# Parameter and constant tables allocated ahead of the weight rings, x and h: every one of those tiles moves by 32 bytes modulo 128

## The chip, the cores and the metric

The kernel runs on one core of one Trainium2 chip. The metric is the device time of one execution in microseconds; each number for a kernel is a median over runs on the chip, and the profile is one profiled execution of the same program.

## What is computed

The reference is two transformer-like blocks over 256 positions and 2048 channels, all in float32. The first has three mixers side by side (pooling, a long convolution done as a Fourier transform, chunked spatial gating) and a feed-forward part; the second has banded attention, an RWKV-7 delta rule and attention to a memory, merged by gates. Cut to the products that take nearly all of the time:

```python
p = rmsnorm(x, norm_mix) @ w_in
x = x + concat([y_a, y_b, y_c]) @ w_out
up = dwconv3(rmsnorm(x, norm_ffn) @ ffn_w_up)
x = x + (silu(gate) * val) @ ffn_w_down
x = rmsnorm(x, norm_final)
proj = rms_norm(x, norm_g) @ w_in_2            # heads, queries, gates
mk, mv = split(rms_norm(mem, mem_norm_g) @ w_mem_kv)
merged = sum(sigmoid(g_m) * (y_m @ w_up_m) for m in (a, b, c))
out = x + merged @ w_o
```

## The kernel before

Activations lie transposed in SBUF, channels over the 128 partitions, 256 positions along each partition. Weights come from HBM as 736 "units" of 512 KB (128 partitions x 1024 floats), each good for 8 tiles of 128x128. SyncE loads unit after unit into a ring of four buffers `raw`. For each unit ScalarE writes the high half `w_hi` (`split`, line 909: a copy rounded to fp32r), VectorE writes `w_lo = raw - w_hi` (line 1316), and TensorE multiplies: for each weight tile three matmuls of 128x128 weights with 256 moving columns, high by high, high by low and low by high, so 24 matmuls a unit. All matmuls are recorded at line 417. Each matmul has its own weight load, which TensorE runs beside the matmul before it (PEld in the profile). The ring's order is fixed in the code: ScalarE waits until TensorE has used the unit four back, VectorE for ScalarE, TensorE for VectorE, SyncE for VectorE.

What multiplies the weights (the moving operand) lies in one of two places:

- **`h_hi`, `h_lo`**, the normed input in two halves: tiles of their own. Used for w_in, ffn_w_up, w_in_2 with its heads, queries and gates: 3 x 4016 matmuls.
- **the shared area** (called the arena from here on), one stretch of SBUF from `arena_at` on in which `place` puts tiles that take turns: `y_hi/y_lo` (for w_out, 3 x 256 matmuls), `m_hi/m_lo` (ffn_w_down, 3 x 704), `mh_hi/mh_lo` (w_mem_kv, 3 x 256), `ya_hi/ya_lo` (the three up-projections, 3 x 384), `mg_hi/mg_lo` (w_o, 3 x 256). The float32 tiles of the delta rule (`m_a`, `m_Q`, `s_...`) are there too.

The tiles are allocated one behind the other along a partition, each from the next multiple of 32 bytes. `par` has 637 floats (2548 bytes) and `con` 1092 (4368 bytes). The byte addresses that follow (start of the tile within a partition, and that modulo 128) are:

| tiles | before | mod 128 | after | mod 128 |
|---|---|---|---|---|
| `raw0` (first of the rings) | 16512 | 0 | 23456 | 32 |
| `w_hi0` | 32896 | 0 | 39840 | 32 |
| `w_lo0` | 49280 | 0 | 56224 | 32 |
| `x` | 65664 | 0 | 72608 | 32 |
| `h_hi`, `h_lo` | 82048, 98432 | 0 | 88992, 105376 | 32 |
| `par`, `con` | 114816, 117376 | 0 | 16512, 19072 | 0 |
| arena | 121760 | 32 | 121760 | 32 |

All moving tiles in the arena start at a multiple of 1024 bytes from its start, and a unit's or tile's parts are 512 or 1024 bytes apart, so each of these matmuls has the offset modulo 128 of its row in the table.

Of the kernel before, what the change touches and what calls it, by code (L numbers as in the profile page):

```python
# [26 lines left out]
P = 128  # L27
# [44 lines left out]
NPAR = _at  # L72
# [11 lines left out]
NCONST = _at  # L84
# [82 lines left out]
def build(nc, a):  # L167
    out_ap = a["out"]
    with ExitStack() as ctx:
        def sb(name, shape, dt=F32):  # L170
            return ctx.enter_context(nc.sbuf_tensor(name, shape, dt))
# [4 lines left out]
        banks = [ctx.enter_context(nc.psum_tensor(f"bank{i}", [P, 512], F32)) for i in range(8)]  # L176


        raw = [sb(f"raw{i}", [P, UK, UN]) for i in range(RING)]
        w_hi = [sb(f"w_hi{i}", [P, UK, UN], F32R) for i in range(RING)]  # L180
        w_lo = [sb(f"w_lo{i}", [P, UK, UN], F32R) for i in range(RING)]
        x = sb("x", [P, KT, T])
        h_hi = sb("h_hi", [P, KT, T], F32R)
        h_lo = sb("h_lo", [P, KT, T], F32R)
        par = sb("par", [P, NPAR])
        con = sb("con", [P, NCONST])
        arena_at = nc.sbuf_base
        arena_at = (arena_at + 31) // 32 * 32
        usable = nc.sbuf_usable_end - arena_at
# [1949 lines left out]
```

How the kernel before makes its waits and increments, by code:

```python
        @block.gpsimd  # L387
        def _(pool):
            for dst, src in ((feat[:, :], "feat"), (fw1[:, :], "fw1"), (fw2[:, :], "fw2")):
                pool.dma_start(dst, a[src]).then_inc(filt_in, 16)
            pool.wait_ge(landed[1], 16)
            for dst, src in ((fw3[:, :], "fw3"), (decay[:, :, :], "decay"), (dft[:, :, :, :], "dft")):
                pool.dma_start(dst, a[src]).then_inc(tables_in, 16)
            pool.wait_ge(free_early, 1)
            for dst, src in ((ws[:, :, :], "ws"), (pw[:, :, :], "pw"), (bs[:, :], "bs")):
                pool.dma_start(dst, a[src]).then_inc(mixer_in, 16)
            pool.wait_ge(free_inv, 1)
            pool.dma_start(inv[:, :, :], a["inv"]).then_inc(inv_in, 16)
            pool.wait_ge(free_lora, 1)
            pool.dma_start(lora[:, :], a["lora"]).then_inc(lora_in, 16)
            with pool.Fori(0, HEADS_A) as g:
                pool.wait_ge(bias_used, g + 1)
                pool.dma_start(bias_t[:, :], a["bias"][g]).then_inc(bias_in, 16)
            pool.wait_ge(free_mem, 1)
            for c in range(4):
                cs = slice(4 * c, 4 * c + 4)
                pool.dma_start(memx[:, cs, :], a["memT"][:, cs, :]).then_inc(mem_in[c], 16)
# [10 lines left out]
            def unit(bank, k0, hi, lo, first, last, tiles=2, fresh=True):  # L419
                slot = next(slots) % RING
                pe.wait_ge(split_done, n.next("split"))
                o = p2(bank)
                for kk in range(UK):
                    for t in range(tiles):
```

## Time and profile before

| | |
|---|---|
| median of 3 runs | 2538.08 us (2537.49 to 2540.97) |
| profiled execution, first to last instruction | 2537.8 us (the page gives no other time of its own) |
| TensorE busy | 2455.0 us, 97% |
| VectorE, ScalarE busy | 1534.1 us, 60%; 1185.9 us, 47% |
| DMA | 400.39 MB, mean 158 GB/s |

Busy time of an engine counts stretches in which at least one of its instructions ran. TensorE's matmuls overlap in the profile (one lasts 0.28 us and the next begins 0.12 us after it), so the length of one is not its cost; the distance between two starts is.

### The profile page before, as it was taken

The page shows a single profiled execution, that of the slowest core. Times are in us where ns is not written, and L with a number is a line of the kernel's source. Part 1 is how long each engine was busy: PE and PEld are TensorE (multiplying, and loading weights), DVE is VectorE, ACT ScalarE, POOL GpSimd, SP SyncE. Part 2 cuts the span into 40 slices and gives each one's busy share as a digit, 9 for nine tenths or more (in the row PEclk, how much of TensorE's full clock was granted, in tenths as well). Part 3 has the DMA queues.
Part 4 walks back from the last instruction along what each step waited for, and adds up shares of the span by engine and source line. Part 5 has one row for each costly group of instructions (what it writes and reads, how often), then busy time and mean ns, then how long its engine had stood idle before and what let it go on. Part 6 is the DMA issues. An engine that isn't in the chain of part 4 may idle for free.

```text
span 2537.8 us, 51128 instructions
## 1 busy us (share of the span) xinstructions
PE 2455.0 (97%) x19960; PEld 2413.6 (95%) x19960; DVE 1534.1 (60%) x2050; ACT 1185.9 (47%) x1502; POOL 12.8 (1%) x27
## 2 busy tenths in 40 slices
PE   6999998999999999997899999999999999999999
PEld 6898997999999999996899999999999999999999
DVE  6456566666555666566866666766576454544454
ACT  5343335665434666434444445444465443434433
POOL 0000000000000000000000000000000000000000
PEclk9999898999999999998999999999999999999999
DMA  6353354555554555554333333333355355555554
GB/s 233 130 180 116 129 187 132 188 170 194 183 186 167 183 181 189 179 185 147 117 119 112 109 120 111 119 123 104 118 175 173 125 184 179 185 176 175 184 187 160
DMA packets 110145, 400.39 MB, mean 158 GB/s; under 512 B 12394, under 2 KB 12421, under 8 KB 109904
## 3 DMA queue, kind: packets, MB, share of 16 engines
q1 hardware_dynamic: 108000, 391.00, 46.4%
q0 software_dynamic: 2032, 7.67, 0.9%
q8 instruction: 97, 1.59, 0.3%
q14 instruction: 16, 0.13, 0.0%
HBM read 396.52 MB, written 2.10 MB: 157 GB/s over the span
## 4 chain that ended last, share of the span: by engine, by line
PE 92%; DVE 5%; issue 1%; ACT 1%; DMA 0%; DVEq 0%; SPq 0%; ACTq 0%
PE bank L417 91%; DVE w_lo L1316 1%; ACT w_hi L909 1%; DVE scratch L1365 1%; PE bank L611 0%; DVE s_k L1365 0%; DVE h_lo L1362 0%; DMA x<-in_xT 0%; DVE cum L1362 0%; DVE root L1404 0%; DVE ping L1362 0%; DVE s_t L1362 0%; DVE qr L1807 0%; DVE acc L1362 0%; DVE s_t L1369 0%
## 5 line engine op out<-in xcount | busy, mean ns | idle before, releaser
L1316 DVE TENSOR_TENSOR w_lo<-raw,w_hi 128x1024 fp32r<-128x1024 f32 x736 | 892.0, 1224 | 803.8 <-ACT w_hi L909 797.5
L909 ACT ACTIVATE w_hi<-raw 128x1024 fp32r<-128x1024 f32 x736 | 770.7, 1057 | 1018.7 <-PE bank L417 999.5
L417 PE MATMUL bank<-h_hi,w_hi 128*128 128x256 f32 x4016 | 1163.3, 290 | 36.6 <-DVE h_lo L1362 15.0
L417 PE MATMUL bank<-h_lo,w_hi 128*128 128x256 f32 x4016 | 1141.0, 284 | 0.0
L417 PE MATMUL bank<-h_hi,w_lo 128*128 128x256 f32 x4016 | 1140.8, 284 | 0.0
L417 PEld LDWEIGHTS bank<-h_hi,w_hi 128*128 128x128 f32 x4016 | 775.6, 193 | 47.0 <-issue 24.4
L417 PEld LDWEIGHTS bank<-h_lo,w_hi 128*128 128x128 f32 x4016 | 775.9, 193 | 3.3 <-issue 2.2
L417 PEld LDWEIGHTS bank<-h_hi,w_lo 128*128 128x128 f32 x4016 | 775.0, 193 | 0.0
L417 PE MATMUL bank<-m_hi,w_lo 128*128 128x256 f32 x704 | 197.8, 281 | 0.0
L417 PE MATMUL bank<-m_hi,w_hi 128*128 128x256 f32 x704 | 197.1, 280 | 0.0
L417 PE MATMUL bank<-m_lo,w_hi 128*128 128x256 f32 x704 | 195.7, 278 | 0.0
L417 PEld LDWEIGHTS bank<-m_hi,w_hi 128*128 128x128 f32 x704 | 132.4, 188 | 0.0
L417 PEld LDWEIGHTS bank<-m_lo,w_hi 128*128 128x128 f32 x704 | 132.4, 188 | 0.0
L417 PEld LDWEIGHTS bank<-m_hi,w_lo 128*128 128x128 f32 x704 | 132.2, 188 | 0.0
L417 PE MATMUL bank<-ya_hi,w_lo 128*128 128x256 f32 x384 | 107.9, 281 | 0.0
L417 PE MATMUL bank<-ya_hi,w_hi 128*128 128x256 f32 x384 | 107.6, 280 | 0.0
L417 PE MATMUL bank<-ya_lo,w_hi 128*128 128x256 f32 x384 | 106.8, 278 | 0.0
L1365 DVE SCALAR_TENSOR_TENSOR conv_o<-bank,par,conv_o 128x255 f32<-128x255 f32 x176 | 76.7, 478 | 6.5 <-DVE conv_o L1365 3.3
L417 PE MATMUL bank<-mh_hi,w_hi 128*128 128x256 f32 x256 | 74.5, 291 | 5.1 <-DVE mh_lo L1362 3.4
L417 PEld LDWEIGHTS bank<-ya_hi,w_hi 128*128 128x128 f32 x384 | 72.3, 188 | 0.0
L417 PEld LDWEIGHTS bank<-ya_lo,w_hi 128*128 128x128 f32 x384 | 72.3, 188 | 0.0
L417 PE MATMUL bank<-mh_hi,w_lo 128*128 128x256 f32 x256 | 72.2, 282 | 0.0
(414 smaller groups left out, 2820.2 us busy)
## 6 DMA issues: line engine op xcount, KB each, us to landing
raw<-in_units SPq DMA_DIRECT2D x736, 512.0 KB, 3.4
x<-in_xT SPq DMA_DIRECT2D x4, 512.0 KB, 5.8
memx<-in_memT POOLq DMA_DIRECT2D x4, 512.0 KB, 7.2
out_y<-obuf SPq DMA_DIRECT2D x8, 256.0 KB, 4.3
bias_t<-in_bias POOLq DMA_DIRECT2D x8, 192.0 KB, 2.9
dft<-in_dft POOLq DMA_DIRECT2D x1, 1024.0 KB, 7.6
decay<-in_decay POOLq DMA_DIRECT2D x1, 768.0 KB, 5.6
con<-in_con SPq DMA_DIRECT2D x1, 546.0 KB, 7.8
```

What stands on the lines that cost most here:

```text
L417: return pe.matmul(out, lhsT, rhs, start=start, stop=stop, skip_group_check=True)
L909: return act.activation(out, in_, ACT.Copy, scale=scale)
L1316: dve.tensor_tensor(w_lo[slot][:, :, :], raw[slot][:, :, :], w_hi[slot][:, :, :].bitcast(F32), ALU.subtract).then_inc(split_done, 1)
L1365: return dve.scalar_tensor_tensor(out, x_, s, y_, op0, op1)
```

## The change

Two lines move to the head of the allocation. No instruction, wait or transfer is added, removed or moved: on each of the five engines the order of instructions is the same in both kernels. What differs is the address of the rings, of `x`, `h_hi`, `h_lo`, and of the two tables. The total size of what stands ahead of the arena is the same, so the arena starts where it did.

```diff
@@ build @@
+        par = sb("par", [P, NPAR])
+        con = sb("con", [P, NCONST])
         raw = [sb(f"raw{i}", [P, UK, UN]) for i in range(RING)]
         w_hi = [sb(f"w_hi{i}", [P, UK, UN], F32R) for i in range(RING)]
         w_lo = [sb(f"w_lo{i}", [P, UK, UN], F32R) for i in range(RING)]
         x = sb("x", [P, KT, T])
         h_hi = sb("h_hi", [P, KT, T], F32R)
         h_lo = sb("h_lo", [P, KT, T], F32R)
-        par = sb("par", [P, NPAR])
-        con = sb("con", [P, NCONST])
         arena_at = nc.sbuf_base
         arena_at = (arena_at + 31) // 32 * 32
```

## Rows read from the trace of the kernel before

**Rows 1.** The page: span, busy time, clock by slices, chain that ended last.

```profile
span 2537.8 us, 51128 instructions
PE 2455.0 (97%) x19960; PEld 2413.6 (95%) x19960; DVE 1534.1 (60%) x2050; ACT 1185.9 (47%) x1502; POOL 12.8 (1%) x27
...
PEclk9999898999999999998999999999999999999999
...
PE 92%; DVE 5%; issue 1%; ACT 1%; DMA 0%; DVEq 0%; SPq 0%; ACTq 0%
```

**Rows 2.** Waits of PE, ACT and SP's queue: total us, times, longest.

```profile
PE bank L417 <- DVE h_lo L1362: 15.0, 2, 8.0
PE bank L417 <- DVE w_lo L1316: 7.2, 5, 2.5
...
ACT w_hi L909 <- PE bank L417: 999.5, 567, 13.3
...
SPq L891 <- DVE w_lo L1316: 2055.1, 732, 26.6
```

**Rows 3.** Groups of matmuls by form: busy us, mean ns of one.

```profile
L417 PE MATMUL bank<-h_lo,w_hi 128*128 128x256 f32 x4016 | 1141.0, 284 | 0.0
...
L417 PE MATMUL bank<-m_lo,w_hi 128*128 128x256 f32 x704 | 195.7, 278 | 0.0
...
L417 PE MATMUL bank<-ya_lo,w_hi 128*128 128x256 f32 x384 | 106.8, 278 | 0.0
...
L417 PE MATMUL bank<-mh_lo,w_hi 128*128 128x256 f32 x256 | 72.1, 282 | 0.0
...
L417 PE MATMUL bank<-y_lo,w_hi 128*128 128x256 f32 x256 | 71.2, 278 | 0.0
...
L417 PE MATMUL bank<-mg_lo,w_hi 128*128 128x256 f32 x256 | 71.2, 278 | 0.0
```

**Rows 4.** Windows: from:to, length, PE busy (matmuls), clock, DMA share, GB/s.

```profile
330.00:380.00 50.00, 50.00 (x426) 1.00 0.54 184
655.00:775.00 120.00, 120.00 (x1021) 1.00 0.56 186
430.00:630.00 200.00, 200.00 (x1669) 1.00 0.55 183
2446.00:2530.00 84.00, 84.00 (x715) 1.00 0.55 181
1928.00:1937.00 9.00, 9.00 (x80) 1.00 0.43 128
1940.00:1949.00 9.00, 9.00 (x79) 1.00 0.50 153
```

**Rows 5.** Weight loads by form, as rows 3.

```profile
L417 PEld LDWEIGHTS bank<-h_lo,w_hi 128*128 128x128 f32 x4016 | 775.9, 193 | 3.3 <-issue 2.2
...
L417 PEld LDWEIGHTS bank<-m_lo,w_hi 128*128 128x128 f32 x704 | 132.4, 188 | 0.0
...
L417 PEld LDWEIGHTS bank<-m_Q,m_b 128*128 128x128 f32 x128 | 15.6, 192 | 0.0
```

**Rows 6.** Timeline of PE after a break in the delta rule: start us, us.

```profile
1448.41 0.49 PE L417 MATMUL bank<-S,m_b 128*128 128x128 f32 x2 [0.40 <-DVE S L1368]
...
1448.86 0.28 PE L417 MATMUL bank<-h_lo,w_hi 128*128 128x256 f32 x1
...
1450.05 0.28 PE L417 MATMUL bank<-h_hi,w_lo 128*128 128x256 f32 x1
```

**Rows 7.** VectorE and ScalarE by tile: duration ns min/median/max, first and last start.

```profile
L1362 DVE TENSOR_TENSOR h_lo<-scratch,h_hi x12: 1217/1219/1226, 21.5 to 1185.3; 128x1024 fp32r<-128x1024 f32 x12
...
L1362 DVE TENSOR_TENSOR mh_lo<-scratch,mh_hi x4: 1219/1222/1226, 1896.2 to 1912.4; 128x1024 fp32r<-128x1024 f32 x4
...
L909 ACT ACTIVATE w_hi<-raw x736: 1038/1059/1091, 15.2 to 2523.4; 128x1024 fp32r<-128x1024 f32 x184
...
L909 ACT ACTIVATE mh_hi<-scratch x4: 1057/1058/1060, 1894.8 to 1911.3; 128x1024 fp32r<-128x1024 f32 x4
```

## The prediction

> **What bounds the kernel now.** I read the page first: TensorE is busy for 97% of the span, and the chain that ended last is TensorE for 92% [rows 1]. Then the waits, to see whether something feeds it late. ScalarE waits 999.5 us for TensorE to give a weight buffer back, and the loading queue waits 2055.1 us for VectorE's split; against that TensorE waits 7.2 us in all for split weights, and its longest total is 15.0 us at the norms [rows 2]. So loads and splits run ahead and are held back by TensorE. The kernel's time is the number of matmuls times the distance between two starts, plus some short waits. A change of addresses can matter in three ways: that distance, the length of the splits, the transfers. Only the first has no cover.
>
> Then I asked whether the distance is the same for all matmuls of one shape, since the two kinds of moving operand stand at different offsets modulo 128. They are of the same form (128x128 weights, 256 columns), yet their mean lengths differ: 284 ns for `h_lo`, 278 ns for `m_lo`, `ya_lo`, `y_lo` and `mg_lo`; `mh_lo` has 282 ns, a mean that takes in some at a low clock [rows 3]. The length only hints. The distance comes from windows in which TensorE is never idle and the clock is 1.00, its 2.4 GHz level [rows 4]. A window counts every matmul that touches it, so the distance is (window + length of one) / count:
>
> - `h`, 430 to 630 us: 200.28 / 1669 = 120.0 ns
> - `m`, 655 to 775: 120.28 / 1021 = 117.8 ns
> - `y`, 330 to 380: 50.28 / 426 = 118.0 ns
> - `mg`, 2446 to 2530: 84.28 / 715 = 117.9 ns
> - `mh`, 1928 to 1937 and 1940 to 1949: 18.56 / 159 = 116.7 ns
>
> The same matmul with the same kind of weights costs 2.2 ns less when its moving operand is in the arena (3.3 ns less for `mh`). Load on the other engines does not explain it: the DMA share is 0.55 for `h` and 0.56 for `m`. The table of addresses gives a candidate. Weights stand at 0 modulo 128 in the kernel before; `h` at 0 too, the arena at 32. **The slow pairs are those in which weights and moving operand have the same offset, the fast ones those in which they differ.** The weight load runs beside a matmul, and its length shows the same split, 193 ns next to `h`, 188 ns next to `m` [rows 5].
>
> The rule of the Trainium skill that speaks against all this is in SBUF — State Buffer, section "Who interferes with whom": TensorE has two SBUF read ports, one for the moving operand and one for the weight load, "independent". By that rule an address changes nothing and the sum would be zero, a time of 2538. The trace does not agree as it stands: one shape of matmul has two distances, 120.0 and 117.8 ns, at full clock.
>
> **The change, part by part.** The rings and `h` go from 0 to 32, the arena stays at 32. No instruction moves, so nothing is queued anew behind anything.
>
> *Matmuls on `h`* (3 x 4016): weights and moving operand move together, their difference stays 0. If the difference decides, they stay at 120.0 ns: cost 0.
>
> *Matmuls on the arena*: the difference goes from 32 to 0. They should take the distance that `h` has now. `y`, `m`, `ya`, `mg` are 3 x (256 + 704 + 384 + 256) = 4800 matmuls. For `ya` no long window is free of `h`; its length of 278 ns is that of `m`, so I give it `m`'s distance. 4800 x 2.2 ns = 10.6 us. `mh`, 3 x 256 = 768 matmuls, x 3.3 ns = 2.5 us. Sum 13.1 us. From below, if such a matmul only goes halfway, 6 us; from above, if all in the arena were at `mh`'s distance today, 5568 x 3.3 = 18 us. I take 13.1, since it is measured group by group. None of it is covered: in these stages ScalarE and VectorE wait for TensorE.
>
> *The float32 matmuls of the delta rule* have weights and operand both in the arena (both at 32): nothing moves. They matter as a witness for a pair with both at 32, the state in which all will be. Their weight loads last 192 ns (`m_Q`), close to the 193 of `h` and not to the 188 of `m` [rows 5]. So "both at 32" looks like "both at 0". The witness is weak, since these are matmuls of another form.
>
> *`h` after a break.* In the delta rule small matmuls cut the stream. After one, from 1448.86 to 1450.05 us, ten distances sum to 1.19 us where the steady ones make 1.20 [rows 6]: 0.01 us is gained until the steady distance is back. Some hundred breaks make 1 us. If the pairing at the break changes, this could be lost, or doubled: bounds -1 to +1, taken as 0.
>
> *Splits and other elementwise work.* VectorE's subtraction over 1024 floats takes 1219 ns with `h_hi` and `h_lo` at 0, and 1222 ns with all three operands at 32; ScalarE's copy takes 1059 ns from ring to ring at 0 and 1058 ns at 32 [rows 7]. No effect, and the splits have the cover named above anyway. Bounds: 3 ns on 736 splits is 2 us of VectorE time beside TensorE. If the cover were gone it would be these 2 us.
>
> *Transfers.* The 32 bytes may cost a queue something. The loading queue waits 2055.1 of 2537.8 us for a free buffer [rows 2], so a load longer by even a tenth stays hidden; only the first loads are bare, and a tenth of them would be under 1 us. Taken as 0.
>
> Sum: 0 + 13.1 + 0. The profiled span, 2537.8 us, is 0.3 below the median of the runs shown, so the sum goes on the median: 2538.1 + 13.1 = 2551.
>
> **Rivals.**
>
> *No change* (2538; 0.15). The distance would not hang on the offset modulo 128 but on something that stays: how far apart the operands are in SBUF, or the code around them. For it: `mh` and `m` have the same offsets and still differ by 1.1 ns, so the offset is not all there is, and the rule quoted above would have it so. Against it: `y`, `m` and `mg` are far apart in SBUF, used by different code, and agree within 0.2 ns.
>
> *Faster* (0.12). The moving operand's own offset decides: 0 is slow, 32 is fast, whatever the weights have. Then `h` drops to the arena's 117.8 ns and the arena stays: 12048 x 2.2 = 26.5 us less, 2512. The point from which it decides is whether a pair with both at 32 is fast. For it: before the change every fp32r matmul with an operand at 32 is fast. Against it: the 192 ns of the delta rule's weight loads, with both at 32. If only the unsettled part of `h` got faster, the gain would be a piece of this.
>
> *Slower by more* (0.08). The offset of 32 of the weights costs something of its own, on top. No row shows weights of this form at 32. If it were as large as the effect seen here, 2.2 ns, on `h` alone, it would add 26 us and give 2577.
>
> **How the numbers follow.** The forecast case has 0.65; its own range is 2544 to 2557 (half of the effect, to all at 3.3 ns). The runs shown differ by 3.5 us, and about 0.2% or 5 us is what a measurement of this kernel can tell from no change. Slower holds the forecast and the last rival: 0.73. Same 0.15, faster 0.12. For 8 in 10 the range must take in the forecast case and no change, hence 2536 to 2558.
>
> **What the profile after would show.** Windows over the same stages: 120.0 ns in `m`, `y`, `mg` and `mh` as in `h`, thus 1002 matmuls in 120 us of the first `m` stage where now there are 1021; the lengths of `m_lo` and `ya_lo` at 283 and not 278 ns; their weight loads at 192. `h` at 120.0 ns and 192 as now. VectorE's and ScalarE's lengths the same. The prediction is wrong if `h` changes its distance at all, since it holds two thirds of the matmuls and 1 ns there is 12 us; or if `m` stays at 117.8.

## The result, and the profile after

| | before | after |
|---|---|---|
| median of the runs | 2539.99 us (2537.49 to 2543.29, 5 runs) | 2549.95 us (2549.65 to 2553.69, 5 runs) |
| ratio | | 1.0042, 95% interval 1.0029 to 1.0054 |
| profiled execution | 2537.8 us | 2548.0 us |
| TensorE busy | 2455.0 us | 2464.3 us |

The change makes the kernel 10 us slower; 2551 was forecast from 2538.1, a loss of 13. The interval of the ratio, times 2540, is a loss of 7 to 14 us.

The windows of the kernel after, over the stages that [rows 4] shows for before (columns: from:to, length, TensorE busy with the number of matmuls, clock, DMA share, GB/s). The stages from the attention on start up to 10 us later, so the windows there are moved: the fourth is in `mg`, the fifth and sixth are in `mh`, and the last takes in `h` and `ya` in turn.

```profile
330.00:380.00 50.00, 50.00 (x419) 1.00 0.55 183
655.00:775.00 120.00, 120.00 (x1002) 1.00 0.57 185
430.00:630.00 200.00, 200.00 (x1669) 1.00 0.55 183
2456.00:2540.00 84.00, 84.00 (x702) 1.00 0.51 178
1933.00:1942.00 9.00, 9.00 (x77) 1.00 0.40 117
1945.00:1952.00 7.00, 7.00 (x61) 1.00 0.27 90
2030.00:2125.00 95.00, 95.00 (x794) 1.00 0.51 173
```

`h` has its 1669 matmuls in 200 us as before. `m` has 1002 in 120 us where it had 1021, and 120.28 / 1002 is 120.0 ns; `y`, 50.28 / 419, and `mg`, 84.28 / 702, give 120.0 and 120.1. `mh` has (16 + 0.56) / 138 = 120.0 ns, from two short windows, and `h` and `ya` together 95.28 / 794 = 120.0. The tile of `mh` shows the same in its lengths (minimum, median and maximum in ns):

```profile
L417 PE MATMUL bank<-mh_lo,w_hi x256: 278/283/418, 1906.6 to 2018.1; 128*128 128x256 f32 x128
```

The median matmul lasts 283 ns, the length that goes with 120.0 ns in the other stages of this kernel. The groups of after by form (busy us, mean ns of one) answer to [rows 3] and [rows 5]:

```profile
L417 PE MATMUL bank<-h_lo,w_hi 128*128 128x256 f32 x4016 | 1140.4, 284 | 0.0
L417 PE MATMUL bank<-m_lo,w_hi 128*128 128x256 f32 x704 | 199.2, 283 | 0.0
L417 PE MATMUL bank<-ya_lo,w_hi 128*128 128x256 f32 x384 | 108.7, 283 | 0.0
...
L417 PEld LDWEIGHTS bank<-m_lo,w_hi 128*128 128x128 f32 x704 | 135.2, 192 | 0.0
```

`m` and `ya` went from 278 to 283 ns and the weight loads of `m` from 188 to 192, so that next to nothing is left of the difference between arena and `h`. The long waits and the splits of after, against [rows 2] and [rows 7]:

```profile
PE bank L417 <- DVE w_lo L1316: 4.9, 4, 2.4
...
ACT w_hi L909 <- PE bank L417: 1009.7, 567, 11.9
...
SPq L891 <- DVE w_lo L1316: 2064.7, 732, 26.6
...
L1362 DVE TENSOR_TENSOR h_lo<-scratch,h_hi x12: 1215/1218/1226, 21.7 to 1188.6; 128x1024 fp32r<-128x1024 f32 x12
...
L909 ACT ACTIVATE w_hi<-raw x736: 1038/1058/1092, 15.4 to 2533.4; 128x1024 fp32r<-128x1024 f32 x184
```

VectorE and ScalarE work as fast at 32 as at 0 (1218 for 1219 ns, 1058 for 1059). ScalarE and the loading queue wait some 10 us longer, since TensorE takes that much longer.

### The profile page after: what moved, and what is told of

The parts are those of the page before. It is cut to its first block, busy times and chain, and to the rows that moved or that the text cites. A ratio compares the mean times of both kernels' runs of the same rounds, so it can differ in the third digit from the quotient of the medians.

```text
span 2548.0 us, 51128 instructions
## 1 busy us (share of the span) xinstructions
PE 2464.3 (97%) x19960; PEld 2424.2 (95%) x19960; DVE 1533.6 (60%) x2050; ACT 1185.3 (47%) x1502; POOL 12.8 (1%) x27
## 4 chain that ended last, share of the span: by engine, by line
PE 92%; DVE 5%; issue 1%; ACT 1%; DMA 0%; DVEq 0%; SPq 0%; ACTq 0%
PE bank L417 91%; DVE scratch L1365 1%; DVE w_lo L1316 1%; ACT w_hi L909 1%; PE bank L611 1%; DVE h_lo L1362 0%; DVE s_k L1365 0%; DMA x<-in_xT 0%; DVE cum L1362 0%; DVE root L1404 0%; DVE ping L1362 0%; DVE s_t L1362 0%; DVE acc L1362 0%; DVE s_t L1369 0%; DVE s_k L1362 0%
## 5 line engine op out<-in xcount | busy, mean ns | idle before, releaser
L417 PEld LDWEIGHTS bank<-ya_hi,w_lo 128*128 128x128 f32 x384 | 73.7, 192 | 0.0
```

The costliest lines, as they stand in the source:

```text
L417: return pe.matmul(out, lhsT, rhs, start=start, stop=stop, skip_group_check=True)
```

## The experiments

"Difference" below is the moving operand's address minus the weights', modulo 128 bytes. Each distance is worked out as in the prediction, (window + 0.28) / count. A count that is off by one moves it by some 0.1 ns in a window of 100 us or more and by 0.3 in one of 50.

**The parameter table alone first.** Rings, x and h shift by 2560 bytes, 20 x 128; all differences stay.

```diff
+        par = sb("par", [P, NPAR])
         raw = [sb(f"raw{i}", [P, UK, UN]) for i in range(RING)]
...
         h_lo = sb("h_lo", [P, KT, T], F32R)
-        par = sb("par", [P, NPAR])
         con = sb("con", [P, NCONST])
```

> Only the parameter table moves to the front. Rings, x and h shift by 2560 bytes, which is 0 modulo 128; the arena stays at 32. Theory (the difference modulo 128 between weights and moving operand decides): nothing changes, 2538 to 2541, arena matmuls at 117.8 ns, h at 120.0. Rival (the distance in SBUF as such, or the difference modulo 512 or more, decides; it changes from 288 to 288 modulo 512 only where 2560 is a multiple, and modulo 1024 from 800 to 288): the arena's distances change, towards 120.0 ns and 2550.

Measured: ratio to before 1.0007 (0.9997 to 1.0016). Windows of `h` and of both `m` stages:

```profile
430.00:630.00 200.00, 200.00 (x1669) 1.00 0.57 184
660.00:760.00 100.00, 100.00 (x852) 1.00 0.57 187
1050.00:1150.00 100.00, 100.00 (x851) 1.00 0.57 186
```

`m` stays at 100.28 / 852 = 117.7 ns, `h` at 120.0. A shift of this size does nothing, so the distance between the operands as such is out, and so is their difference modulo 1024, which changed. But 2560 is also 5 x 512, so the difference modulo 256 and modulo 512 stayed as it was. No run here changes it by 128 alone: that the period is 128 and not 256 or 512 is assumed in this document, not shown.

**Only x and h go to 32.** The constant table stands between the rings and x.

```diff
         w_lo = [sb(f"w_lo{i}", [P, UK, UN], F32R) for i in range(RING)]
+        con = sb("con", [P, NCONST])
         x = sb("x", [P, KT, T])
...
         par = sb("par", [P, NPAR])
-        con = sb("con", [P, NCONST])
```

> Rings stay at 0, x and h go to 32, arena stays at 32 (the constant table stands between them). Theory (difference decides): all 17616 matmuls are now at difference 32. With the arena's present 117.8 ns for h: 12048 x 2.2 = 26.5 us less than before, about 2513; if h enters its stages from a break and holds the 116.7 ns of mh, up to 12048 x 3.3 + 4800 x 1.1 = 45 us less, 2495. Rival (the weights' own offset is what made the arena slow in the changed kernel, the operand's own offset nothing): h stays at 120.0 ns and the time at 2540.

Measured: 2506.75 us beside 2537.63, ratio 0.9880 (0.9862 to 0.9899), 31 us faster than before. Windows for each half of the feed-forward part, first in the up-projection (`h`) alone, then on into the down-projection (`m`) with no pause of TensorE between the two:

```profile
430.00:630.00 200.00, 200.00 (x1717) 1.00 0.57 186
430.00:760.00 330.00, 330.00 (x2831) 1.00 0.58 189
800.00:1000.00 200.00, 200.00 (x1701) 1.00 0.56 187
800.00:1100.00 300.00, 300.00 (x2550) 1.00 0.57 188
```

`h` is at 116.6 ns in the first half and 117.7 in the second, not at 120.0, and `m` goes on as `h` did: over both, the windows give 330.28 / 2831 = 116.7 and 300.28 / 2550 = 117.8. This beats both kernels of the study. Its four runs lie 9 us apart (2503.16 to 2512.02), where before lies 7 apart in the same session (2534.24 to 2541.73).

**Only the rings go to 32.** x, h and the constant table are allocated ahead of them, so h is at 0 with a difference of 96, and the arena has 0.

```diff
+        x = sb("x", [P, KT, T])
+        h_hi = sb("h_hi", [P, KT, T], F32R)
+        h_lo = sb("h_lo", [P, KT, T], F32R)
+        con = sb("con", [P, NCONST])
         raw = [sb(f"raw{i}", [P, UK, UN]) for i in range(RING)]
         w_hi = [sb(f"w_hi{i}", [P, UK, UN], F32R) for i in range(RING)]
         w_lo = [sb(f"w_lo{i}", [P, UK, UN], F32R) for i in range(RING)]
-        x = sb("x", [P, KT, T])
-        h_hi = sb("h_hi", [P, KT, T], F32R)
-        h_lo = sb("h_lo", [P, KT, T], F32R)
         par = sb("par", [P, NPAR])
-        con = sb("con", [P, NCONST])
```

> Rings at 32, h at 0, arena at 32. Theory (difference decides): the arena is at difference 0, as slow as in the changed kernel, 120.0 ns; h is at a difference of -32, that is 96, for which no row stands: 117 to 118 ns if the sign does not matter, giving 2550 - 26 = 2524 or less. Rival (weights at 32 are slow by themselves, whatever the operand): h stays at 120.0 and the time at 2550.

Measured: ratio 0.9980 (0.9970 to 0.9989), 5 us faster.

```profile
430.00:630.00 200.00, 200.00 (x1692) 1.00 0.56 186
660.00:760.00 100.00, 100.00 (x836) 1.00 0.57 184
```

With the weights at 32, `h` at 0 is at 118.4 ns and `m` at 32 is at 120.0. In the kernel before it was the other way round. So neither operand's own offset, 0 or 32, decides; their difference does. The size was missed (2524 or less was expected, 2532 measured), since 96 is not as good as 32: 12048 x 1.6 is 19 us, less the arena's 13.

**Difference 64.** As the second run, with 32 unused bytes between the constant table and x.

```diff
+        con = sb("con", [P, NCONST])
+        pad = sb("pad", [P, 8])
         x = sb("x", [P, KT, T])
```

> Rings at 0; x, h and the arena all at 64 (constant table and 32 unused bytes between). Theory: a difference of 64 is not 0, so all matmuls are fast, as in the run with h at 32, 2495 to 2513. Rival (what counts is the difference modulo 64): the difference is 0 again, all at 120.0 ns, 2550.

Measured: 2514.32 us, ratio 0.9910 (0.9892 to 0.9927), 1 us above the range expected. It is not slow, so the rule is not one modulo 64. Unlike all before, `h` has two far apart distances, seen in a window near the start and in one of the first up stage:

```profile
100.00:150.00 50.00, 50.00 (x444) 1.00 0.59 197
430.00:630.00 200.00, 200.00 (x1700) 1.00 0.56 186
```

50.28 / 444 is 113.2 ns and 200.28 / 1700 is 117.8. The timeline (start us, length us) of two entries into the same group of matmuls, the first after the small sums of the query stage, the second after those and the sum over the memory, shows where they part:

```profile
1845.31 0.47 PE L418 MATMUL bank<-h_hi,w_hi 128*128 128x256 f32 x1
1845.62 0.28 PE L418 MATMUL bank<-h_lo,w_hi 128*128 128x256 f32 x1
...
1846.30 0.28 PE L418 MATMUL bank<-h_lo,w_hi 128*128 128x256 f32 x1
```

```profile
1857.92 0.47 PE L418 MATMUL bank<-h_hi,w_hi 128*128 128x256 f32 x1
1858.23 0.28 PE L418 MATMUL bank<-h_lo,w_hi 128*128 128x256 f32 x1
...
1860.23 0.28 PE L418 MATMUL bank<-h_hi,w_hi 128*128 128x256 f32 x1
```

The first goes on with six distances in 0.68 us (113 ns), the second with seventeen in 2.00 us (118 ns). Such a stretch takes one of two rhythms when it starts and keeps it (the "state" of the expectations below).

**Differences 16, 48, 80, 96 for all.** All tiles at fixed addresses (a small spare tile moves within the arena too). For 16, 48 and 80 the `w_hi` and `w_lo` rings are slices that begin 16 bytes into one tile, which starts at 0, while x, h and the arena start at 32, 64 or 96; for 96 the rings are at 0. The kernel for 16:

```diff
-        w_hi = [sb(f"w_hi{i}", [P, UK, UN], F32R) for i in range(RING)]
-        w_lo = [sb(f"w_lo{i}", [P, UK, UN], F32R) for i in range(RING)]
+        w = at("w", [P, 2 * RING * UK * UN + 8], 32896, F32R)
+        def part_of_w(i):
+            s = 4 + i * UK * UN
+            return w[:, s:s + UK * UN].rearrange("p (k n) -> p k n", k=UK)
+        w_hi = [part_of_w(i) for i in range(RING)]
+        w_lo = [part_of_w(RING + i) for i in range(RING)]
...
+        h_hi = at("h_hi", [P, KT, T], 86560, F32R)
+        h_lo = at("h_lo", [P, KT, T], 102944, F32R)
...
-        arena_at = nc.sbuf_base
-        arena_at = (arena_at + 31) // 32 * 32
+        arena_at = 121888
```

> Weights at 16, x, h and arena at 32 modulo 128: difference 16 for every fp32r matmul. Theory A (only an exact difference of 0 modulo 128 is slow; the two streams then keep step): 116.7 to 117.8 ns, 2500 to 2515. Theory B (the difference counts in steps of 32 bytes, 16 falls in with 0): 120.0 ns, 2550.

> Weights at 16, the rest at 64: difference 48. Theory A: fast as at 32 and 64, 113.3 to 117.8 ns by the state in which a stretch starts, 2440 to 2515. Theory B: as at 32, 116.7 to 117.8 ns, 2500 to 2515. With 64 it also tells whether the state of 113.3 ns seen in part of the stretches at 64 is there at its neighbours.

> Weights at 16, the rest at 96: difference 80. If the effect is symmetric round 64, as 48: 2440 to 2515. If it depends on the sign, other distances than at 48.

> Weights at 0, the rest at 96: difference 96 for all. The run with the rings alone at 32 had h at this difference and 118.3 ns: then 118.3 ns everywhere, 12048 x 1.7 - 4800 x 0.5 - 768 x 1.6 = 17 us below before, about 2521. Rival (what counts in that run was the weights' own offset of 32, worth some ns): then weights at 0 give less, 116.7 to 117.8 ns, 2500 to 2513.

Ratios to before: 16: 1.0055 (1.0038 to 1.0072); 48: 0.9977 (0.9968 to 0.9987); 80: 0.9970 (0.9948 to 0.9992); 96: 0.9958 (0.9942 to 0.9975). In time only 16 did what one of its theories said. The others lie above their ranges: 2533.94 us at 48 and 2529.46 at 80, for ranges that end at 2515, and 2528.23 at 96 for 2521. The window of `h` from 430 to 630 us in each, in that order, a fence for each kernel:

```profile
430.00:630.00 200.00, 200.00 (x1669) 1.00 0.54 181
```

```profile
430.00:630.00 200.00, 200.00 (x1688) 1.00 0.56 187
```

```profile
430.00:630.00 200.00, 200.00 (x1701) 1.00 0.56 189
1050.00:1150.00 100.00, 100.00 (x847) 1.00 0.56 187
2020.00:2110.00 90.00, 90.00 (x732) 1.00 0.52 180
```

```profile
430.00:630.00 200.00, 200.00 (x1693) 1.00 0.56 188
660.00:760.00 100.00, 100.00 (x847) 1.00 0.56 187
```

| difference | 0 | 16 | 32 | 48 | 64 | 80 | 96 |
|---|---|---|---|---|---|---|---|
| ns from start to start | 120.0 | 120.0 | 116.6 or 117.8 | 118.6 | 113.2 or 117.8 | 117.7, 118.4 or 123.3 | 118.3 |

The third window of 80 is in the merge stage: 90.28 / 732 = 123.3 ns for `h` and `ya` alike, at full clock and with TensorE never idle. It is the longest distance of this study, at a difference that is far from 0. The ten runs of this kernel go from 2523.36 to 2548.81 us, so the ratio of 80 is that of a mixture; that the share of the long rhythm is what differs from run to run is likely, but only one was traced.

Theory A falls at 16, which is as slow as 0. Theory B's step of 32 bytes does not hold above it: 48 differs from 32. Both readings leave a rival: in the kernels for 16, 48 and 80 the weights themselves start at 16, not at a multiple of 32, and no run has weights at 16 with a difference known from elsewhere. What their own offset costs there is not tested. At 96 the rings at 0 give 118.3 ns for `h`, as 118.4 with the rings at 32: again only the difference shows, and the rival of that run, an own cost of weights at 32, falls. The 16 here is 144 modulo 256 (86560 - 32912 = 53648); 0 and 144 are both slow, which does not tell a period of 128 from one of 256.

**Breaks ahead of the long stretches.** One small matmul, of which nothing is used, runs 13 times (ahead of the up and the down stage of both halves, twice in each of the four merge rounds, ahead of the last stage); once with difference 64 and once in the kernel before.

```diff
+            def short_break():
+                mm(banks[7][0:64, 0:T], con[0:33, 0:64], con[0:33, 0:T])
...
+                short_break()
                 with n.loop(FF_HALF // 2, ...):
...
+                short_break()
                 for q in range(4):
...
+                        if m3 == 1:
+                            short_break()
                         group(0, h_hi, h_lo)
...
+            short_break()
             with n.loop(4, {("fill", 0): 1, ("fill", 1): 1, "split": 8}):
                 group(0, mg_hi, mg_lo, ready=(merged_ready, (6, 6, 6, 8)))
```

> The kernel with difference 64, and one small matmul (33 rows, 64 columns, result unused) ahead of both halves' up and down stages, in the merge stage and ahead of the last one: 13 in all, some 0.3 us each, 4 us. Theory (a stretch keeps, to its end, the state in which it is entered, and such a matmul enters the one of 113.3 ns, as it did twice at the start of the run with difference 64): about 14000 matmuls go from 117.8 to 113.3 ns, 63 us less than that run's 2514, plus 4: 2455. Rival (the state depends on the nanosecond of the entry or on the stage): some stretches stay at 117.8, 2455 to 2518.

> The kernel before with the same small matmuls. Theory (mh is at 116.7 ns and m at 117.8 only because m is entered from a running stretch of h and mh from a break): m and mg now run at 116.7 ns, ya, still entered from h, stays at 117.8, h at 120.0; the time is 2 x 704 x 3 / 2 ... that is 2880 matmuls x 1.1 = 3 us less and 4 us more: 2538 to 2541. Rival (the places of the tiles make the difference): m and mg stay at 117.8.

Difference 64 with breaks: median 2505.94 us, but 2488.48 to 2512.74 over four runs, ratio 0.9846 (0.9802 to 0.9891). Its windows in the first stage, the w_out stage, the last stage and the first `m`, and behind them the w_out stage of the run above without breaks:

```profile
100.00:150.00 50.00, 50.00 (x427) 1.00 0.55 181
290.00:370.00 80.00, 80.00 (x708) 1.00 0.60 196
2430.00:2500.00 70.00, 70.00 (x620) 1.00 0.55 187
660.00:760.00 100.00, 100.00 (x851) 1.00 0.57 188
```

```profile
290.00:370.00 80.00, 80.00 (x681) 1.00 0.57 189
```

113.4 ns in the w_out stage and the last one, 117.8 in the first `m`, though the same break stands ahead of the last stage and of `m`. So a stretch behind a break can have the shorter rhythm but does not have to: the forecast of 2455 fails, the rival with it stands. The first two windows lie ahead of all breaks, where both kernels of difference 64 have the same instructions and addresses. Yet the first stage is at 117.8 here and at 113.2 without breaks, and w_out at 113.4 here and 117.9 there. These are two programs, each traced once, that part only further on; so the addresses and what runs ahead of a stretch do not fix its rhythm alone.

The kernel before with breaks, the first `m` and the last stage:

```profile
660.00:760.00 100.00, 100.00 (x859) 1.00 0.56 185
2460.00:2540.00 80.00, 80.00 (x688) 1.00 0.54 181
```

100.28 / 859 and 80.28 / 688 are both 116.7 ns, where [rows 4] has 117.8 and 117.9. That is `mh`'s distance. Same tiles and same addresses, another entry, and `m` and `mg` run like `mh`. A break is no guarantee of it: with h alone at 32 the second half also starts behind a pause and has 117.7.

The single run took 2549.98 us, 9 above what was expected. Its trace accounts for this. A break was taken to cost 0.3 us, and it costs more, here ahead of the first `m`:

```profile
652.28 0.28 PE L417 MATMUL bank<-h_hi,w_lo 128*128 128x256 f32 x1
652.49 0.64 PE L417 MATMUL bank<-con 33*64 33x256 f32 x2
653.06 0.39 PE L417 MATMUL bank<-m_hi,w_hi 128*128 128x256 f32 x1
653.28 0.28 PE L417 MATMUL bank<-m_lo,w_hi 128*128 128x256 f32 x1
```

From 652.28 to 653.28 us there is 1.00 us where two distances make 0.24, so the break costs 0.76 us. Eleven of the 13 stand in a running stream (the two ahead of the up stages fall into a wait): 8.4 us. The last three merge rounds, 2130 to 2450 us, have a granted clock of 0.98 where before has 1.00, an estimate of some 5 us. Less 3.2 us for 2880 matmuls at 1.1 ns, that is about 10 us, and the profiled execution is 10.5 us longer than that of before (2548.3 and 2537.8).

## Why the prediction was right

**What bounds the kernel.** Right: TensorE's stream. A longer distance came out in the time, and the waits of the others grew with it.

**Difference, not place or own offset.** Right, for own offsets of 0 and 32. The changed kernel shows it for difference 0 with both at 32; the run with only the rings at 32 shows `h` fast at its old offset and `m` slow at its own; the run with only h at 32 turns 10 us of loss into 31 us of gain.

**`h` stays at 120.0 ns.** Right, 1669 in 200 us in both kernels. The weak witness, the delta rule's weight loads of 192 ns, pointed the right way, but such a length does not always go with the distance: at difference 16 `m` is at 120.0 ns and its loads last 189:

```profile
L425 PEld LDWEIGHTS bank<-m_lo,w 128*128 128x128 f32 x704 | 132.9, 189 | 0.0
```

**The arena goes to `h`'s distance.** Right within 0.1 ns for `y`, `m`, `mg` and `mh`, and for `ya` together with `h`. The term of 13.1 us stands in the count of matmuls; 10.0 was measured, and 13.1 lies inside the interval. In the profiled pair the loss is 10.2 us. The mean granted clock of that pair differs, 0.985 before and 0.987 after, which is worth up to 0.002 x 2548 = 5 us the other way. The runs of after with a clock of 0.985 bear this out: their spans are 2550.5 and 2552.0 us, 12.7 and 14.2 above the 2537.8 that before took at 0.985. So the 3 us between forecast and measurement are best put down to the clock, which the prediction took as equal. The run with difference 16 has the same 120.0 ns everywhere and came 14 us above before.

**Splits and transfers at 0.** Right: the medians of ScalarE's and VectorE's rows moved by 1 ns. What `h` gains after a break was not measured by itself.

**The rivals.** "No change" is refuted by the ratio and by the counts of `m`, `y`, `mg` and `mh`. It stood on a rule of the Trainium skill (SBUF — State Buffer, section "Who interferes with whom"): the moving operand and the weight load have independent ports. The prediction read it to say that addresses do not count; the runs have 120.0 ns at one difference and 113.2 at another, and the measurement decides. Whether the two ports are where it happens is not shown. The argument of this rival that `mh` and `m` differ at one offset is answered by the kernel before with breaks. "Faster" would have needed `h` at 117.8; it stayed. "Slower by more" would have needed it above 120.0; weights at 32 cost nothing that shows by themselves.

Left open: what in the memory makes the two reads meet. That they do is argued from the weight load beside each matmul, 188 ns in the kernel before and 192 in the slow one after; the 189 ns at difference 16 speak against it as a measure, and no run takes the weight load away. Open too is why the faster streams give back less than their count: with h alone at 32 the two windows promise (3.4 + 2.3) / 2 x 12048 = 34 us for `h`, and 31 were measured in all (33 in the profiled pair). Open are also the period of the rule and the own part of weights at 16, as said above, and what chooses the rhythm at an entry.

## What to carry to other kernels

Where TensorE is the bound and each matmul has its own weight load, compare the distance of two starts between stages of one form; 2 to 3 ns there times 12048 matmuls were worth 31 us here. Then look at the addresses of weights and moving operand modulo 128: here 0 and 16 apart cost 120.0 ns, 32 apart 116.6 to 117.8, and one table put between two tiles was worth 1.2%. Time such a kernel over several runs and look at more than one stretch: at 80 apart one window had 117.7 ns and another 123.3. A change that "only" reorders allocations must be timed like any other, and one that shifts two operands together must be checked against the third that stays.

## What was not expected of the hardware

A stretch of matmuls without a pause keeps the rhythm in which it starts, through a change of the moving tile: 2831 matmuls at 116.7 ns and 2550 at 117.8, both at difference 32. At 64 it is 113.2 or 117.8 ns, at 80 117.7, 118.4 or 123.3. At 0 and 16 all stretches looked at settle on 120.0. The runs of such a kernel scatter: by 24 us at difference 64 with breaks (2488.48 to 2512.74, four runs) and by 25 us at 80 (ten runs), where the kernel before scatters by 5.5 in the session of the former (2537.75 to 2543.24). At 64 without breaks four runs scatter by 8.

All this is seen at full clock alone. At the low level of the clock (granted 0.50, 1.2 GHz, in the trace of the kernel before from 390.00 to 400.70 us) the starts of the matmuls on `h` are farther apart:

```profile
397.72 0.42 PE L417 MATMUL bank<-h_lo,w_hi 128*128 128x256 f32 x1
...
400.71 0.35 PE L417 MATMUL bank<-h_hi,w_hi 128*128 128x256 f32 x1
```

Fourteen distances sum to 2.99 us, 214 ns each, and half of that is 107 ns; every distance measured at full clock is above it. The address costs nothing that shows at this level: with h alone at 32 seventeen distances sum to 3.63 us there (391.92 to 395.55 us), 214 ns each too, where at full clock the two kernels differ by 2 to 3 ns a matmul.
